# Gate and up of an expert pair as two sweeps of 256 columns, each with its own loads

## The reference

```python
for every expert e, on the tokens xb routed to it (6 of 64 experts a token):
    h = jax.nn.silu(xb @ w_gate[e]) * (xb @ w_up[e])     # 1024 -> 256, twice
    acc[tok] += (h @ w_down[e]) * w                       # 256 -> 1024
```

## Time and profile before

| | |
|---|---|
| median of three executions | 1301.03 us |
| profiled execution, its own time | 1303.12 us |
| its span | 1301.3 us |
| PE busy | 1194.9 us, 92% |
| mean granted TensorE clock | 0.976 |
| read from memory | 442.63 MB, 341 GB/s over the span |
| experts of layer 0 on PE | about 191 to 658 us |
| experts of layer 1 on PE | about 816 to 1282 us |

### The profile page before, as it was taken

One profiled execution on the slowest core, in us unless ns is written; L12 is line 12 of the kernel. 1 busy time (PEld: TensorE's weight loads), 2 busy tenths in 40 slices (PEclk: granted clock), 3 DMA queues, 4 the chain that ended last, 5 costly groups with the idle time before them and its releaser, 6 DMA issues.

```text
span 1301.3 us, 16051 instructions
## 1 busy us (share of the span) xinstructions
PE 1194.9 (92%) x6187; PEld 540.2 (42%) x6187; DVE 368.0 (28%) x746; ACT 256.9 (20%) x546; POOL 16.0 (1%) x22
## 2 busy tenths in 40 slices
PE   7999899999999999999879989999999999999984
PEld 3555453434344343434235645343434434343431
DVE  0575561212122121212142456221202212121213
ACT  1332321212011111111114532111101111111110
POOL 0000000000000000000000000000000000000000
PEclk9997999999999999999979999999999999999997
DMA  9535349999999999999980445899999999999992
GB/s 344 143 146 211 125 176 375 418 420 419 402 376 420 421 419 421 420 420 421 421 339 35 194 164 213 309 419 420 420 418 361 421 419 420 421 420 421 421 419 91
DMA packets 68896, 444.39 MB, mean 341 GB/s; under 512 B 7792, under 2 KB 12272, under 8 KB 18544
## 3 DMA queue, kind: packets, MB, share of 16 engines
q1 hardware_dynamic: 68848, 443.71, 84.3%
HBM read 442.63 MB, written 1.05 MB: 341 GB/s over the span
## 4 chain that ended last, share of the span: by engine, by line
PE 70%; DMA 20%; DVE 4%; ACT 2%; issue 2%; SPq 2%; POOL 1%; POOLq 0%; DVEq 0%
PE psum L849 28%; DMA ring<-in_expert_w_up 18%; PE psum L872 11%; PE psum L801 5%; PE psum L967 3%; PE psum L898 3%; PE psum L693 3%; PE psum L585 2%; PE psum L729 2%; DMA ring<-in_swa_nsa_w_in 2%; PE psum L1108 2%; PE psum L707 1%; SPq L351 1%; PE psum L882 1%; PE psum L638 1%
## 5 line engine op out<-in xcount | busy, mean ns | idle before, releaser
L849 PE MATMUL psum<-ring,arena 128*64 128x512 f32 x2016 | 460.6, 603 | 32.1 <-DMA ring<-in_expert_w_up 31.9
L849 PEld LDWEIGHTS psum<-ring,arena 128*64 128x64 f32 x2016 | 157.0, 139 | 326.2 <-issue 272.8
L872 PE MATMUL psum<-ring,room 128*64 128x512 f32 x1008 | 233.8, 597 | 2.2 <-ACT room L1286 0.9
L1803 DVE TENSOR_TENSOR y_low<-psum,y_high 128x1024 fp32r<-128x1024 f32 x64 | 78.4, 1225 | 366.7 <-ACT y_high L1272 366.7
L1794 DVE SCALAR_TENSOR_TENSOR room<-room,arena,psum 128x256 f32<-128x256 f32 x64 | 30.8, 481 | 373.0 <-ACT room L1279 373.0
L872 PEld LDWEIGHTS psum<-ring,room 128*64 128x64 f32 x1008 | 75.8, 136 | 129.5 <-issue 120.0
L1272 ACT CAST y_high<-psum 128x1024 fp32r<-128x1024 f32 x64 | 64.8, 1012 | 252.3 <-PE psum L872 252.3
L1279 ACT ACTIVATE room<-psum 128x256 f32<-128x256 f32 x64 | 24.6, 384 | 421.3 <-PE psum L849 421.3
L898 PE MATMUL psum<-y_high,spread 32*128 32x512 f32 x512 | 65.2, 499 | 5.0 <-issue 4.8
L801 PE MATMUL psum<-onehot,x_high 128*128 128x256 f32 x256 | 65.7, 297 | 0.0
L801 PE MATMUL psum<-onehot,x_low 128*128 128x256 f32 x256 | 63.0, 284 | 0.0
(11 more groups left out here) (237 smaller groups left out, 890.9 us busy)
## 6 DMA issues: line engine op xcount, KB each, us to landing
ring<-in_expert_w_down SPq DMA_DIRECT2D x126, 1024.0 KB, 16.1
ring<-in_expert_w_gate SPq DMA_DIRECT2D x122, 1024.0 KB, 14.3
ring<-in_expert_w_up SPq DMA_DIRECT2D x122, 1024.0 KB, 16.4
ring<-in_swa_nsa_w_in SPq DMA_DIRECT2D x8, 1036.0 KB, 13.8
room<-in_swa_nsa_w_out SPq DMA_DIRECT2D x2, 2048.0 KB, 7.9
ring<-in_expert_w_gate SPq DMA_DIRECT2D x8, 512.0 KB, 7.4
ring<-in_expert_w_up SPq DMA_DIRECT2D x8, 512.0 KB, 8.5
room<-in_mla_w_out SPq DMA_DIRECT2D x1, 4096.0 KB, 20.5
```

The costliest lines, as they stand in the source:

```text
L849: mm = pe.matmul(BANK[2][CAP * e:CAP * e + CAP, :], xg[:, c, 2 * j + e, :], expert(stored[e])[0][:, c], start=c == 0, stop=c == KC - 1)
L872: mm = pe.matmul(PS[0][CAP * e:CAP * e + CAP, half * 512:(half + 1) * 512], ht[:, c, CAP * e:CAP * e + CAP], expert(stored[e])[1][:, c, ha ...
L1803: V.tensor_tensor(ylo, PS[0][:, :], yhi.bitcast(F32), ALU.subtract).then_inc(sem[f"yd_dve{L}"], 1)
```

## The change

Gate and up are computed one after the other: for each of the two, 8 chunks of 256 moving columns for each expert, gate into the left half of bank 2 and up into bank 3. Each has its own semaphores for its loads and its own refill; the halves of the first refill are gone. silu starts after the gate sweep. The turned h goes to the right half of bank 2 in place of bank 3. As up needs bank 3, it waits for `gates_dve`; gather and slots change places on PE, and `x_gathered` and `gates_in` on DVE.

```diff
             def refill(i, kept=None):
                 for j in range(NPAIR):
                     mine = [k for k in (2 * j, 2 * j + 1) if k != kept]
-                    if isinstance(i, int) and i == 0 and j == 0:
-                        for half in range(2):
-                            sp.wait_ge(sem[f"gu_pe{L}"], 2 * half + 2)
-                            for k in mine:
-                                expert_half(sp, L, k, NSLOT + k, half)
-                    else:
-                        sp.wait_ge(sem[f"gu_pe{L}"], (i * NPAIR + j + 1) * 4)
-                        for k in mine:
-                            expert_gate_up(sp, L, k, ((i + 1) * NSLOT + k) % NE)
+                    sp.wait_ge(sem[f"gu_pe{L}"], (i * NPAIR + j) * 4 + 2)
+                    for k in mine:
+                        expert_gate(sp, L, k, ((i + 1) * NSLOT + k) % NE)
+                    sp.wait_ge(sem[f"gu_pe{L}"], (i * NPAIR + j) * 4 + 4)
+                    for k in mine:
+                        expert_up(sp, L, k, ((i + 1) * NSLOT + k) % NE)
...
 def pe_slots
-                pe.wait_ge(sem[f"ht_act{L}"], p)
+                pe.wait_ge(sem[f"h_dve{L}"], p + 1)
...
 def pe_gate_up
-            halves = 64 if j % NPAIR == 0 and not (isinstance(turn, int) and turn == 0) else 0
-            pe.wait_ge(sem[f"gu{j % NPAIR}_in{L}"], (turn + 1) * 64 + halves - 32 * missing(i, j, beyond))
+            there = (turn + 1) * 32 - 16 * missing(i, j, beyond)
+            pe.wait_ge(sem[f"ga{j % NPAIR}_in{L}"], there)
...
-            for c in range(KC):
-                if first:
-                    pe.wait_ge(sem[f"{'xg_dve' if c % 2 else 'xg_act'}{L}"], c // 2 + 1)
-                for e in range(2):
-                    mm = pe.matmul(BANK[2][CAP * e:CAP * e + CAP, :], xg[:, c, 2 * j + e, :],
-                                   expert(stored[e])[0][:, c], start=c == 0, stop=c == KC - 1)
-                    if c % 4 == 3:
-                        mm.then_inc(sem[f"gu_pe{L}"], 1)
+            for m in range(2):
+                if m:
+                    pe.wait_ge(sem[f"up{j % NPAIR}_in{L}"], there)
+                    pe.wait_ge(sem[f"gates_dve{L}"], i + 1)
+                for c in range(KC):
...
+                    for e in range(2):
+                        mm = pe.matmul(BANK[2 + m][CAP * e:CAP * e + CAP, 0:DE], xg[:, c, 2 * j + e, :],
+                                       expert(stored[e])[0][:, c, m, :], start=c == 0, stop=c == KC - 1)
+                        if c == KC - 1:
+                            mm.then_inc(sem[f"gu_pe{L}"], 1)
...
-        def pe_turn(pe, L, p, gates):
-            pe.wait_ge(sem[f"gates_dve{L}"], gates)
+        def pe_turn(pe, L, p, gathered):
             pe.wait_ge(sem[f"h_dve{L}"], p + 1)
+            if gathered is not None:
+                pe.wait_ge(sem[f"xg_dve{L}"], gathered * 4 + 3)
             for c in range(2):
-                mm = pe.transpose(BANK[3][:, c * P:(c + 1) * P], hh[:, c, :], ident)
+                mm = pe.transpose(BANK[2][:, DE + c * P:DE + (c + 1) * P], hh[:, c, :], ident)
...
                     if ahead:
+                        pe_gather(pe, L, i + 1, p)
                         pe_slots(pe, L, i + 1, p)
-                        pe_gather(pe, L, i + 1, p)
...
             def silu(p):
-                act.wait_ge(sem[f"gu_pe{L}"], (p + 1) * 4)
+                act.wait_ge(sem[f"gu_pe{L}"], p * 4 + 2)
...
                     dve.wait_ge(sem[f"silu_act{L}"], p + 1)
+                    dve.wait_ge(sem[f"gu_pe{L}"], p * 4 + 4)
...
-                    V.scalar_tensor_tensor(hh, byc(sg), gslot[:, j, 0:1], byc(BANK[2][:, DE:2 * DE]),
+                    V.scalar_tensor_tensor(hh, byc(sg), gslot[:, j, 0:1], byc(BANK[3][:, 0:DE]),
...
                         if j == GP - 1 and not last:
+                            x_gathered(i + 1)
                             gates_in(i + 1)
-                            x_gathered(i + 1)
```

More of the change, by code:

```diff
@@ L117 @@
 EACH = ["pick_dve", "slots_pe", "gates_dve", "gather_pe", "xhi_act", "xlo_dve", "xg_act", "xg_dve",
-        "gu_pe", "silu_act", "h_dve", "spread_dve", "ht_pe", "ht_act", "down_pe", "ya_act", "yd_dve", "half_pe", "comb_pe"] + [f"{part}{k}_in" for part in ("gu", "dn") for k in range(NPAIR)]
+        "gu_pe", "silu_act", "h_dve", "spread_dve", "ht_pe", "ht_act", "down_pe", "ya_act", "yd_dve", "half_pe", "comb_pe"] + [f"{part}{k}_in" for part in ("ga", "up", "dn") for k in range(NPAIR)]
 SEMS = (
@@ L357, in one, with expert_gate, expert_up @@
             return w[L, bass.ds(e, 1)].rearrange("a k n -> (a k) n")
-        def expert_gate_up(sp, L, k, e):
[L360 to L367, removed]
+        def expert_gate(sp, L, k, e):
+            sp.dma_start(slot[k][:, 0:KC * DE], one(e_gate, L, e).rearrange("(p c) f -> p (c f)", c=KC))\
+              .then_inc(sem[f"ga{k // 2}_in{L}"], 16)
+        def expert_up(sp, L, k, e):
+            sp.dma_start(slot[k][:, KC * DE:2 * KC * DE], one(e_up, L, e).rearrange("(p c) f -> p (c f)", c=KC))\
+              .then_inc(sem[f"up{k // 2}_in{L}"], 16)
+        def expert_gate_up(sp, L, k, e):
+            expert_gate(sp, L, k, e)
+            expert_up(sp, L, k, e)
         def expert_down(sp, L, k, e):
@@ L844, in pe_gate_up @@
                 pe.wait_ge(sem[f"h_dve{L}"], p)
-            for c in range(KC):
-                if first:
-                    pe.wait_ge(sem[f"{'xg_dve' if c % 2 else 'xg_act'}{L}"], c // 2 + 1)
-                for e in range(2):
-                    mm = pe.matmul(BANK[2][CAP * e:CAP * e + CAP, :], xg[:, c, 2 * j + e, :],
-                                   expert(stored[e])[0][:, c], start=c == 0, stop=c == KC - 1)
-                    if c % 4 == 3:
-                        mm.then_inc(sem[f"gu_pe{L}"], 1)
+            for m in range(2):
[3 more added lines that the diff above has]
+                for c in range(KC):
+                    if first:
+                        pe.wait_ge(sem[f"{'xg_dve' if c % 2 else 'xg_act'}{L}"], c // 2 + 1)
+                    for e in range(2):
[3 more added lines that the diff above has]
+                            mm.then_inc(sem[f"gu_pe{L}"], 1)
         def pe_down(pe, L, i, j, last, beyond):
@@ L923, in group @@
                     if ahead:
+                        pe_gather(pe, L, i + 1, p)
                         pe_slots(pe, L, i + 1, p)
-                        pe_gather(pe, L, i + 1, p)
                     if not first:
                         pe_combine(pe, L, p - 1, before, 0)
-                    pe_turn(pe, L, p, i + 2 if ahead else i + 1)
+                    pe_turn(pe, L, p, i + 1 if ahead else None)
                     if not first:
@@ L1285, in turned @@
                     act.wait_ge(sem[f"down_pe{L}"], p * 2)
-                nc.scalar.copy(ht, v(BANK[3][:, 0:2 * P], c=2, t=P)).then_inc(sem[f"ht_act{L}"], 1)
+                nc.scalar.copy(ht, v(BANK[2][:, DE:DE + 2 * P], c=2, t=P)).then_inc(sem[f"ht_act{L}"], 1)
             for tc in range(TC):
```

## The result

The changed kernel takes 1280.72 us (median of 4, 1278.01 to 1280.99) against 1300.45 us (median of 4) of the kernel before on the same chip: a ratio of 0.9845, interval 0.983 to 0.9861. Run once more beside other kernels it gave 0.9838, interval 0.9823 to 0.9852. The forecast was 1284 us in a range of 1278 to 1292.

A forecast was written before the change was run, and what follows sets the result against it. DMA was taken to bound the experts, plus times its queue is empty and PE's work after the last bytes; 7.5 + 9.4 = 16.9 us gained took the median 1301.0 to 1284 us, range 1278 to 1292.

The forecast's parts named there:

- DMA bounds the experts, PE has some us a group to spare: Experts, per group of four pairs: weights take DMA 59.9 us, PE's work 55.3 us, so DMA is slower by 4.6 us.
- Streaming adds 0: Gate and up sweeps on PE: 32 added weight loads a pair cost 0; upper bound 1.5 us a pair.
- The dry spell: DMA queue runs empty once a layer after pair 10, losing 4.8 and 4.7 us; 1.0 left, 7.5 us gained in all.
- The first refill goes out at the same time as before: Start of each layer's experts: first refill issued as before, since half the old work and the new gate sweep take 3.5 us.
- The end: Each layer's last up landing to last down: 5.35 us against 10.9, gain taken as 4.7 a layer, 9.4 for both.
- h sooner is hidden: PE's 0.36 us wait ahead of the turn goes in three pairs of four; worth nothing where DMA bounds.
- The sum: Whole kernel: 7.5 + 9.4 = 16.9 us off the profiled execution's 1303.1 us.
- the one of the end alone: Rival: the queue still runs empty as before, only each layer's end is gained; 1291.6 us, chance 0.12.
- the one of a lower rate: Rival: gate, gate, up, up loads move at 412 in place of 420 GB/s, so nothing changes; 1301 us, chance 0.05.
- that of the clock: Rival: the clock falls more often, losing 1.7 us in up and 1.7 in down at each end; 1291 us, chance 0.08.
- that of the weight loads: Rival: added weight loads in the sweeps make PE the bound, slower; 1335 us at 47 ns a load, chance 0.07.

The follow-up runs named there:

- late_silu: The changed kernel, but silu waits for the end of the up sweep and no longer runs beside it; 1280.25 us (0.9849).
- cols128: The changed kernel with each sweep cut in two again, four sweeps of 128 columns a pair, doubling gate and up weight loads; 1285.49 us (0.9892).
- halves_rows: The changed kernel, but each layer's first refill goes out as 8 loads of 512 KB, each with half of every partition's row; 1282.40 us (0.9866).
- halves_apart: The changed kernel with the first refill as 8 half-row loads of 512 KB, first halves of both experts ahead of second halves; 1280.40 us, one execution.
- both_late: The changed kernel, but PE starts gate only when up has landed too, and gate's refill waits for the up sweep (first refill excepted); 1298.93 us (0.9985).
- halves_parts: The changed kernel with the first refill as 8 loads of 512 KB, each with whole rows for half of the partitions; 1297.96 us (0.9972).
- gate_first_down_first: The changed kernel, each layer's first gate sweep ahead of slots and shared turns, loads after the experts held until the last down weights landed; 1277.47 us (0.9818).
- late_start: The changed kernel, but PE starts on gate only when up has landed too; refills stay split; 1289.46 us (0.9929).

## Why the prediction was right, point by point

The forecast of 1284 us was 3.3 us too high: it counted on 17 us and 19.7 came. The repeat, 1278.2, lies at the lower bound of the range. The mechanism was right in the parts that were counted; one term, the start, was put at nothing and wasn't.

- *DMA bounds the experts, PE has some us a group to spare.* Right. late_silu, paid for by PE in every pair, moved the time by nothing that can be told; each loss of bytes at the start came out in full. cols128 is the exception: 0.08 us a pair on PE, and 4.8 us by the medians.
- *Streaming adds 0.* Right: 7.08 us a pair against 7.04.
- *The dry spell, gained 3.8 and 3.7 us.* Right in mechanism; the measured gain is 4.6 and 4.4, as nothing is left of it. I took PE at pair 10 to be 3.5 us sooner. Counted from the first gate, its up ended at 330.65 - 189.8 = 140.9 in place of 337.83 - 191.1 = 146.7 us, 5.9 sooner, 2.5 of them because up's weights came sooner.
- *The first refill goes out at the same time as before, counted as 0.* This is the step that was mis-sized. The time of issue is the same (3.7 us after the first gate), but the old loads moved more slowly: 222 against 282 GB/s over 16 us, 2.3 us a layer. The old trace had it, in the rate of the first stretches, and I had looked at the issue alone. Half rows account for 1.4 of it (halves_rows, halves_apart), and the rest stays open. Layer 1 of both_late shows that a quicker start counts only since the dry spell is gone.
- *The end, 5.35 us from the last up to the last down.* Measured 5.32 in layer 1; 6.41 in layer 0, where down's weights were 1.0 us late, the one thing named as late next. I took 4.7 us a layer for the gain, between a clock that falls and one that doesn't; it didn't fall, and the gains were 4.5 and 5.6.
- *h sooner is hidden.* Right to within what can be told: late_silu shows 0.6 us at the end of layer 1 and some of the lead.
- *The sum.* 16.9 us forecast; 23.2 between the two profiled executions within the experts, 19.7 between the medians. Of the 6.3 us that the sum lacked, 4.5 are the start.
- The rivals: the one of the end alone and the one of a lower rate are ruled out by the flat rates, that of the clock by sweeps of 3.67 us, that of the weight loads by the pair's 7.08 us and by cols128. The rival of the clock was priced 1.7 us too high, as the 4.7 us of each end already held half of what a fallen clock costs.
- *The clock.* My reading that the old kernel's sweeps took 7.09 us everywhere but at the two ends was wrong. Three more were stretched, one in layer 0 (the row below) and two in layer 1 (8.78 us at 1088.09 and at 1192.85), after 2.05 to 2.10 us of idle time. DMA hid them, as PE has time to spare there. In the changed kernel, where that idle time is cut in two, no sweep is stretched: the rival had the direction the wrong way round.

```profile
524.07 8.79 PE L849 MATMUL psum<-ring,arena 128*64 128x512 f32 x32 [2.09 <-DMA ring<-in_expert_w_up]
```

## What to carry to other kernels

Where a queue of loads is the bound, look for the few places where it stands empty, and ask for each whether it is paid at the end: a loss at the start is hidden as long as a later dry spell takes it up (layer 1 of both_late), and comes out in full once that is filled (halves_rows, halves_parts). Two fixes for the same dry spell share it, so undoing one of them shows less than it is worth alone (3 to 4 us for the sooner refill beside PE's early start, 9.5 us without it). Splitting a product by operand lets the engine start on the first half of the bytes and end half a product after the last of them, at no cost in streaming here. Compare rates, not times of issue, when two kernels load the same bytes in different pieces.

## What the runs showed of the hardware that was not expected

- Loads over 64 partitions moved at 217 GB/s, those over 128 at 420, with the DMA engines' share at 1.02 in both: here the busy share doesn't show the rate.
- Eight loads of 512 KB in rows of 4 KB lost 1.4 us over 4.2 MB against four loads of 1 MB in rows of 8 KB.
- The last loads of a queue with nothing behind them ended at half the rate: 221 and 197 GB/s for 2 us (gate_first_down_first).
- The clock: the old kernel's last sweeps were stretched to 8.78 us after 2.12 and 2.18 us of idle time. In late_start the sweeps of two pairs waited 2.55 us each; the earlier ones were stretched to 8.81 us, the last of layer 1 were not, as these rows of its timeline show. The length of the idle time just before a sweep doesn't settle it alone.

```profile
456.69 8.81 PE L853 MATMUL psum<-ring,arena 128*64 128x256 f32 x64 [2.55 <-issue]
...
1254.99 7.13 PE L853 MATMUL psum<-ring,arena 128*64 128x256 f32 x64 [2.55 <-issue]
```
